# The end of a recurrent layer: an output product started among the steps of a norm

## The reference

```
y = _rwkv7_scan(rh, wh, kh, vh, kk, ah)
ym = jnp.mean(y, axis=-1, keepdims=True)
yv = jnp.mean(jnp.square(y - ym), axis=-1, keepdims=True)
y = ((y - ym) * lax.rsqrt(yv + RWKV_GN_EPS)).reshape(bsz, t, B_WIDTH)
y = y * gn_g.astype(jnp.float32) + gn_b.astype(jnp.float32)
bonus = jnp.sum(rh * kh * r_k.astype(jnp.float32), axis=-1, keepdims=True) * vh
y = (y + bonus.reshape(bsz, t, B_WIDTH)) * g.astype(jnp.float32)
...
h = h + jnp.concatenate([ya.astype(h.dtype), yb.astype(h.dtype)], axis=-1) @ e_w_out[i]
hn = _rms_norm(h, e_norm_ffn[i])
h = h + _swiglu(hn, ffn_w_gate[i], ffn_w_up[i], ffn_w_down[i])
```

## Time and profile before

| what | value |
|---|---|
| time, median of 3 runs | 2216.14 us (2215.89 to 2217.43) |
| profiled execution, its own time | 2213.22 us |
| its span | 2211.4 us |
| PE busy | 2061.4 us (93%) |
| DVE busy | 1311.2 us (59%) |
| ACT busy | 1051.0 us (48%) |
| POOL busy | 255.1 us (12%) |
| mean granted PE clock | 0.953 |

### The profile page before, as it was taken

How to read it: one execution, slowest core, us unless ns; L and a number is a source line. 1 busy time by engine, 2 the same in 40 slices (tenths; PEclk the granted TensorE clock), 3 DMA queues, 4 the chain that set the end, 5 groups by cost and what they waited for, 6 DMA issues and landing times.

```text
span 2211.4 us, 33449 instructions
## 1 busy us (share of the span) xinstructions
PE 2061.4 (93%) x13840; PEld 1770.0 (80%) x13840; DVE 1311.2 (59%) x2000; ACT 1051.0 (48%) x1683; POOL 255.1 (12%) x270
## 2 busy tenths in 40 slices
PE   6999989999999899999999879999789899999997
PEld 4775668888778755899988879999677788888886
DVE  1338545666454448577557544454555678888886
ACT  2336533333334326466446324443344566666674
POOL 0300012101100320222013211110100000000000
PEclk9999999999999899999998989999889899999998
DMA  7332443444222121244534014555351477888784
GB/s 298 117 134 96 153 171 115 171 172 171 95 89 83 64 77 58 94 171 177 207 139 148 3 40 144 190 176 188 143 199 43 166 292 304 323 304 323 304 308 150
DMA packets 52671, 364.86 MB, mean 165 GB/s; under 512 B 5920, under 2 KB 8224, under 8 KB 8864
## 3 DMA queue, kind: packets, MB, share of 16 engines
q1 hardware_dynamic: 49488, 357.06, 43.6%
q10 hardware_dynamic: 3024, 5.57, 0.7%
HBM read 361.56 MB, written 1.05 MB: 164 GB/s over the span
## 4 chain that ended last, share of the span: by engine, by line
PE 82%; DVE 9%; ACT 3%; issue 3%; POOL 2%; DMA 1%; SPq 0%; DVEq 0%; POOLq 0%; ACTq 0%
PE ps L77 21%; PE ps L78 20%; PE ps L79 20%; PE ps L74 18%; DVE WLO L91 3%; PE ps L82 2%; ACT R L85 2%; DVE R L91 1%; DVE SM L105 1%; DMA ring<-W 1%; ACT WHI L85 1%; POOL h L95 1%; POOL R L91 1%; DVE x L88 0%; DVE R L96 0%
## 5 line engine op out<-in xcount | busy, mean ns | idle before, releaser
L91 DVE TENSOR_TENSOR WLO<-ring,WHI 128x1024 fp32r<-128x1024 f32 x557 | 670.7, 1239 | 240.9 <-ACT WHI L85 240.2
L85 ACT ACTIVATE WHI<-ring 128x1024 fp32r<-128x1024 f32 x557 | 568.6, 1052 | 130.5 <-PE ps L79 121.1
L77 PE MATMUL ps<-HHI,WHI 128*128 128x256 f32 (+1 forms) x1680 | 550.7, 328 | 33.1 <-DVE HLO L88 15.1
L78 PE MATMUL ps<-HLO,WHI 128*128 128x256 f32 (+1 forms) x1744 | 562.7, 323 | 0.0
L79 PE MATMUL ps<-HHI,WLO 128*128 128x256 f32 (+1 forms) x1680 | 543.6, 324 | 0.0
L77 PEld LDWEIGHTS ps<-HHI,WHI 128*128 128x128 f32 x1680 | 332.5, 198 | 71.4 <-issue 41.5
L78 PEld LDWEIGHTS ps<-HLO,WHI 128*128 128x128 f32 x1744 | 344.8, 198 | 21.0
L79 PEld LDWEIGHTS ps<-HHI,WLO 128*128 128x128 f32 x1680 | 331.9, 198 | 21.9
L74 PE MATMUL ps<-R 64*64 64x64 f32 (+12 forms) x2832 | 247.9, 290 | 9.7 <-DVE R L96 3.9
L74 PEld LDWEIGHTS ps<-R 64*64 64x64 f32 (+5 forms) x2832 | 187.2, 156 | 53.5 <-issue 36.9
L85 ACT ACTIVATE R<-ps 128x512 f32<-128x512 f32 (+5 forms) x255 | 124.0, 489 | 196.6 <-PE ps L74 95.8
(11 more groups left out here) (164 smaller groups left out, 2832.1 us busy)
## 6 DMA issues: line engine op xcount, KB each, us to landing
ring<-W SPq DMA_DIRECT2D x340, 1024.0 KB, 4.9
x<-xt ACTq DMA_DIRECT2D x1, 2048.0 KB, 14.7
CR<-const_nsa ACTq DMA_DIRECT2D x1, 560.0 KB, 4.8
out<-x SPq DMA_DIRECT2D x1, 512.0 KB, 3.0
out<-x ACTq DMA_DIRECT2D x1, 512.0 KB, 3.0
CR<-const_rw ACTq DMA_DIRECT2D x1, 448.0 KB, 3.2
CR<-const_gqa ACTq DMA_DIRECT2D x1, 320.0 KB, 17.0
CR<-const_mla ACTq DMA_DIRECT2D x1, 320.0 KB, 2.9
```

The lines of the kernel that those rows point to most:

```text
L77: self.e.matmul(out, l[0], r[0], start=start, stop=False)
L78: self.e.matmul(out, l[0], r[1], start=False, stop=False)
L85: return self.e.activation(out, in_, func, **kw)
L91: return self.e.tensor_tensor(out, in0, in1, op)
```

## The change

Three streams are rewritten, and no instruction is added or taken away.

- PE: the output product starts after the mean of chunk 1. The variance product stands ahead of step k = 1 and the spreading of the roots ahead of step k = 2.
- ACT and DVE: the splits of the first four units move into the last phase of the solve of chunk 1. On ACT two stand ahead of the WT copy and two between the WT and NU copies. On DVE all four stand ahead of the copy of `y`, with the gate of chunk 0 between the pairs.
- The high and low part of chunk 0 of `yb` are made among the norm steps of chunk 1.

```diff
@@ project_block
         for k in range(K):
+            if step:
+                step(k)
             for ev in needs(k):
@@ solve_act
+            if c:
+                hi_units(a, L["e_out"].first[0:2])
             a.wait_ge(*at("wt_pe", c))
             a.act(WT, bank("wt", c)[:, :], ACT.Copy).then_inc(*did("rhs", ("wt", c)))
+            if c:
+                hi_units(a, L["e_out"].first[2:4])
             a.wait_ge(*at("nu_pe", c))
@@ solve_dve
                 begin(1)
+            else:
+                lo_units(v, L["e_out"].first[0:2])
+                gate_out_dve(v, 0)
+                lo_units(v, L["e_out"].first[2:4])
             v.wait_ge(*at("y_pe", c))
@@ rwkv_out_*
-    def rwkv_out_pe(pe):
-        mean_pe(pe, 1)
-        var_pe(pe, 1)
-        roots_pe(pe, 1)
+    def rwkv_out_steps(pe, k):
+        if k == 0:
+            mean_pe(pe, 1)
+        if k == 1:
+            var_pe(pe, 1)
+        if k == 2:
+            roots_pe(pe, 1)
...
         spread_act(a, 1)
+        y_high_act(a, 0)
         root_out_act(a, 1)
-        for c in range(2):
-            a.wait_ge(*at("yb", c))
-            a.act(HHI[:, 4:8, of_chunk(c)], h[:, 4:8, of_chunk(c)], ACT.Copy).then_inc(*did("h_hi", ("yh", 4 + c)))
+        y_high_act(a, 1)
...
     def rwkv_out_dve(v):
-        gate_out_dve(v, 0)
         centre_dve(v, 1)
+        y_low_dve(v, 0)
         recip_out_dve(v, 1)
         scale_out_dve(v, 1)
         gate_out_dve(v, 1)
+        y_low_dve(v, 1)
@@ pe / act / dve streams
-        rwkv_out_pe(pe)
-        out_pe(pe, "e_out", L["e_out"], 256, hx(0, 256), y_done, 8)
+        out_pe(pe, "e_out", L["e_out"], 256, hx(0, 256), y_done, 8, step=lambda k: rwkv_out_steps(pe, k))
-        hi_units(a, L["e_out"].first)
-        lo_units(v, L["e_out"].first)
```

More of the change, by code:

```diff
@@ L1038, in summed_after, with out_pe @@
         return min(j, 2 * (j - st.side + 1)) if st.side else j
-    def out_pe(pe, key, st, N, X, needs, c, before=None):
+    def out_pe(pe, key, st, N, X, needs, c, before=None, step=None):
         done = 0
         if st.side:
-            project_block(pe, st, [(("group", key, j), ("x", key, j), N, X) for j in range(st.side)], needs)
+            project_block(pe, st, [(("group", key, j), ("x", key, j), N, X) for j in range(st.side)], needs, step)
         for j in range(st.side, 8):
@@ L2482, in rwkv_out_act, with y_high_act, y_low_dve @@
         spread_act(a, 1)
+        y_high_act(a, 0)
         root_out_act(a, 1)
-        for c in range(2):
-            a.wait_ge(*at("yb", c))
-            a.act(HHI[:, 4:8, of_chunk(c)], h[:, 4:8, of_chunk(c)], ACT.Copy).then_inc(*did("h_hi", ("yh", 4 + c)))
+        y_high_act(a, 1)
+    def y_high_act(a, c):
+        a.wait_ge(*at("yb", c))
+        a.act(HHI[:, 4:8, of_chunk(c)], h[:, 4:8, of_chunk(c)], ACT.Copy).then_inc(*did("h_hi", ("yh", 4 + c)))
+    def y_low_dve(v, c):
+        v.wait_ge(*at("yh", 4 + c))
+        v.tt(HLO[:, 4:8, of_chunk(c)], h[:, 4:8, of_chunk(c)], HHI[:, 4:8, of_chunk(c)], ALU.subtract).then_inc(
+            *did("h_lo", ("yl", 4 + c)))
     def rwkv_out_dve(v):
-        gate_out_dve(v, 0)
         centre_dve(v, 1)
+        y_low_dve(v, 0)
         recip_out_dve(v, 1)
```

## The result

| kernel | median of its runs | lowest to highest | runs |
|---|---|---|---|
| before | 2216.01 us | 2215.14 to 2217.43 | 4 |
| changed | 2202.24 us | 2198.46 to 2207.18 | 4 |

The ratio is 0.9944, with a 95% interval of 0.9932 to 0.9955: 10 to 15 us faster. The forecast was 2205.4 us in a range of 2202.5 to 2209.0; the ratio times the 2216.14 us that the forecast started from is 2203.7 us, inside the range, while the plain median lies 3.2 us under the forecast and 0.3 us under the range. Against 5 further runs of the changed kernel and 21 of the one before the ratio was 0.9955 (0.9942 to 0.9969), which is 10 us, and their medians were 2203.95 and 2214.94 us. The profiled execution of the changed kernel was the slowest of its four, 2207.18 us with a span of 2205.3 us.

What follows compares the result with a forecast made beforehand. PE, busy 93% of the span, bounds the kernel; the 8.59 us hole and slow start are targeted. Gains 7.2, 0.8, 0.9 and 2.7 less 0.9 make 10.7 us: 2216.14 to 2205.4 us, range 2202.5 to 2209.0.

Steps and rivals of the forecast that it cites:

- The sum: From the copy of `y` to group 4 of the output product: all steps together gain 10.7 us.
- The fit of the splits: Moved splits fit idle ACT and DVE time in the solve: margins 1.1 us (WT), 0.8 (NU), 1.4 (`y`); cost nothing.
- the bound of 1.55: DVE's low parts of the moved unit splits: at most 1.55 us each.
- The clock: PE's clock in the new order, chiefly after the 1.6 us wait ahead of k = 4: stays 1.00, no loss taken.
- rows 7: Trace rows at 326.70 to 328.90: PE busy 0.62 of 2.20 us between dense matmuls, clock 1.00 there and four microseconds behind.
- The two pure clock terms: Norm of chunk 1 at full clock: variance 1.88 to 1.05 us gains 0.8, spreading 1.97 to 1.09 gains 0.9.
- the slow matmuls: First matmuls of the output product, at clock 0.50 from 1319.40 to 1322.50 before; in the new order none runs slowly.
- The clock falling after the wait: First rival: clock falls behind the wait ahead of k = 4, costing 1.7 us; gain 9.0 us, 2207.1 us; chance 0.2.
- the clock low through the block: Second rival: clock low from the mean through the whole block; gain 0.8 us, 2215.3 us; chance 0.07.
- POOL's low parts late: Fourth rival: POOL's low parts of `ya` come late, over 3 us each, so the early start buys nothing; chance 0.02.
- The third rival: Unit splits ahead of ACT's WT copy wait for weights and delay the solve, lateness less 1.1 us; slower; chance 0.02.
- the term that I bounded by 1.7 us: Clock in the norm following this layer's product, whose idle times fall 10.7 us earlier: 1.7 us in either direction.

Runs made afterwards that it cites:

- PE's order alone: Kernel before with only PE's new order, nothing moved on ACT and DVE; copy of `y` to group 4 27.45 us, total's ratio 0.9998.
- before with the hole filled: Kernel before plus 36 unread filler matmuls between mean and variance and 2 between variance and spreading; copy of `y` to group 4 24.79 us.
- changed, gate late: Changed kernel with the gate of chunk 0 back ahead of centring chunk 1, splits still in the solve; copy of `y` to group 4 21.10 us.
- splits alone: Changed kernel with PE's order as before, ACT and DVE still changed; copy of `y` to group 4 19.00 and 19.18 us, ratio 0.9952.
- roots early: Changed kernel with the spreading of the roots directly behind the variance, ahead of k = 1; copy of `y` to group 4 16.48 us, ratio 0.9946.
- halves: Roots early, plus gate, high and low part of chunk 1 made in two halves of the features; 16.19 us twice, ratio 0.9944 to before.
- The forced case: Changed kernel with all four ACT unit splits ahead of the WT copy; last masks to copy of `y` 14.52 us, 2.43 us more than changed.

## Why the prediction was right

| kernel | to group 4 | less than before |
|---|---|---|
| before, two traces | 27.95, 27.98 | |
| PE's order alone | 27.45 | 0.5 |
| before with the hole filled | 24.79 | 3.2 |
| changed, gate late | 21.10 | 6.9 |
| splits alone, two traces | 19.00, 19.18 | 8.8 to 9.0 |
| changed, two traces | 17.35, 17.36 | 10.6 |
| roots early | 16.48 | 11.5 |
| halves, two traces | 16.19, 16.19 | 11.8 |

**The sum.** 10.7 us were forecast and 10.6 measured inside the stage. Every step lies within 0.15 us of its place, counted from the start of the copy of `y`: centring at 1.94 us (forecast 1.25 behind the copy's end, so 1.94), variance at 3.35 (3.4), spreading at 5.87 (5.84), k = 4 at 11.52 (11.46), group 4 at 17.35 (17.22).

**The fit of the splits.** Right, with nothing lost at the copy of `y`. The low parts took 1.18 us each in place of the bound of 1.55. POOL was idle beside them, where it ran beside those of rows 1. ACT's margin at NU was 0.24 us in place of 0.8, so the fit was closer there than the forecast said.

**The clock.** Its full speed after the 1.50 us wait was the open point, and it held in both traces of the changed kernel. The reason I gave, dense work ahead of the idle as in rows 7, is not enough by itself. The clock held behind 1.50 us after the norm with k = 0 to 3, 9.2 us of work with hardly a break, and fell behind 1.44 and 0.59 us with only two short norm products around them. But with the gate late, the mean and k = 0 stood without a break, 2.56 us at 1.00, ahead of 1.33 us of idle, and the clock fell all the same. How much dense work holds it through how much idle is open. Rows 7 were also a weaker witness than I took them for: over the 4 us ahead of them, 322.70 to 326.70, PE was busy for 3.92 us but the clock was 0.58, so it had only just risen there. That the forecast took no loss was therefore a choice with luck in it. The two pure clock terms, 0.8 and 0.9 us, and the slow matmuls together were tested by the filled hole: 3.16 us against the 3.1 expected.

The Trainium skill's warning (TensorE: Matmul & The Clock Gate, section "A second HAM failure mode: psum-queue depth-cycling"), that cycling through banks with small idles lets the clock fall again and again, did not come true for the changed kernel, at 1.00 for the whole block over four banks. In the splits-only kernel the clock did fall, but ahead of the block, within the second of its two idles, and it rose again while the block ran.

**The rivals.** The clock falling after the wait, the clock low through the block, and POOL's low parts late were all absent. The third rival, ACT late at WT, did not occur either, but its price was wrong. I put one microsecond for each microsecond. The forced case cost 2.43 us for 0.80 us, because behind the longer idle the clock was low for longer under `nu` and `y`.

**The total.** The forecast was 2205.4 us, the median of four 2202.24, of the five later runs 2203.95. The traces show that the stage lies at another time in each execution. In all 14 the instructions up to the last masks of the solve are the same. Still the copy of `y` started anywhere from 1301.90 to 1310.21 us in the 13 that leave WT its place. Taking that start from the execution's time leaves 2213.22 - 1304.51 = 908.71 and 2211.55 - 1301.95 = 909.60 us before, and 2207.18 - 1307.70 = 899.48 and 2203.73 - 1304.08 = 899.65 us after. The pairs differ by 9.6 us, which is 1.0 us less than the local gain.

A part of this last microsecond can be found, and it is the term that I bounded by 1.7 us, the clock in the norm behind the layer. The glu product starts at 1351.74 before and at 1344.30 in the changed kernel, 19.28 and 19.25 us behind the start of group 4. Then its matmuls start 0.21 us apart for 5.2 us before and for 6.3 us after (the first with 0.28 us of duration are at 1356.95 and 1350.57). From there on the changed kernel is 0.4 us later, counted from group 4, and the second trace of each kernel shows the same. The rest, some 0.6 us, can't be told from the 0.9 us by which the two traces of before differ.

The range does not follow from its own terms. A clock stretch of 1.7 us and 1.5 us for the runs are 3.2 us, and the text takes 2.9 below and 1.9 above; with 3.2 the lower end is 2202.2. Either way 1.5 us for the runs was too small: the runs of before alone later spread from 2210.37 to 2218.43 us. That the plain median of four lies 0.3 us under the range, and that of the five later runs inside it, is within this spread.

## What to carry to other kernels

Look for the engine that holds the serial chain between two phases, and move its bulk work into its own idle time ahead of the chain's input, not behind it. Giving PE its work earlier without that brought 0.5 us of 10.6. Check the margins first: the copy of NU was left only 0.24 us. Price a hole of PE as its length and the slow start behind it, and put some of the bulk work between the short steps of a norm even where the filled time is small, because here it kept the clock up (1.65 us for 0.3 us of filled time). It is no guarantee: with the gate late, k = 0 stood there too and the clock fell. When a total spreads by more than the effect, measure a distance between two instructions around the change: it repeated here to 0.2 us.

## What the runs showed of the hardware that was not expected

An idle of PE can cost more than its length. The gate back on the path adds 1.8 us of work and costs 3.75 us, and 0.80 us of further idle ahead of `nu` costs 2.43 us. In both, the granted clock was 0.50 for over 4 us of the work behind the idle. But 1.50 us of idle in the changed kernel and 0.59 us with the roots early left the clock at 1.00. So the length of one idle did not decide it: the clock fell within 0.59 us in the splits-only kernel, where another idle of 1.44 us stood one short product ahead.
